# Modulation of the hybrid layers computed by GpSimd and one-column matmuls inside the feed-forwards, and the last values of stick-breaking moved

## What is computed

```python
def hybrid_layer(x, c, cos, sin, pre_g, post_g, w_ada, b_ada, w_in, w_out):
    mod = jnp.einsum('bd,de->be', jax.nn.silu(c), w_ada) + b_ada      # (1,1024) x (1024,3072)
    shift, scale, gate = jnp.split(mod, 3, axis=-1)
    h = rms_norm_2(x, pre_g) * (1 + scale[:, None, :]) + shift[:, None, :]
    ...
    return x + gate[:, None, :] * y

def swiglu(h, w_gu, w_down):                                          # the feed-forward, width 2816
    g, u = jnp.split(h @ w_gu, 2, axis=-1)
    return (jax.nn.silu(g) * u) @ w_down
```

## Time and profile before

| | us |
|---|---|
| median of three runs (1872.96 to 1873.77) | 1873.28 |
| span of the profiled execution, first to last instruction | 1873.6 |
| TensorE busy in it | 1798.3 (96%) |
| VectorE busy | 1225.3 (65%) |
| ScalarE busy | 1043.2 (56%) |
| GpSimd busy | 68.9 (4%) |
| mean granted TensorE clock | 0.985 of full |
| share of TensorE in the chain that ended last | 88% |

### The profile page before, as it was taken

One profiled execution on the slowest core, in us unless ns is written; L12 is line 12 of the kernel. 1 busy time (PEld: TensorE's weight loads), 2 busy tenths in 40 slices (PEclk: granted clock), 3 DMA queues, 4 the chain that ended last, 5 costly groups with the idle time before them and its releaser, 6 DMA issues.

```text
span 1873.6 us, 41689 instructions
## 1 busy us (share of the span) xinstructions
PE 1798.3 (96%) x17857; PEld 1616.9 (86%) x17857; DVE 1225.3 (65%) x1798; ACT 1043.2 (56%) x1625; POOL 68.9 (4%) x54
## 2 busy tenths in 40 slices
PE   7899999999999999998999999998999999999998
PEld 7798798889989888897788898897798898888887
DVE  7853567865447675498678757763577756765764
ACT  6865465555446555455665547854565544564554
POOL 0001000000000000113000000001000000000000
PEclk9999999999999999999999999999999999999998
DMA  7320255557567655545276563310356565464441
GB/s 223 113 85 3 69 183 192 185 186 243 191 222 247 202 176 189 153 155 188 65 211 199 178 199 99 115 48 4 94 185 195 175 198 174 136 204 122 136 136 67
DMA packets 288526, 287.75 MB, mean 154 GB/s; under 512 B 15240, under 2 KB 286456, under 8 KB 288344
## 3 DMA queue, kind: packets, MB, share of 16 engines
q1 hardware_dynamic: 285048, 283.98, 47.9%
q10 hardware_dynamic: 3296, 1.11, 0.3%
HBM read 284.03 MB, written 1.05 MB: 152 GB/s over the span
## 4 chain that ended last, share of the span: by engine, by line
PE 88%; DVE 4%; ACT 3%; DMA 3%; issue 2%; SPq 0%; DVEq 0%; ACTq 0%
PE ps L412 23%; PE ps L413 12%; PE ps L389 10%; PE ps L391 9%; PE ps L390 9%; PE ps L840 2%; PE ps L429 2%; PE ps L430 2%; PE ps L431 2%; PE ps L816 1%; PE ps L825 1%; PE ps L726 1%; PE ps L740 1%; PE ps L654 1%; PE ps L1009 1%
## 5 line engine op out<-in xcount | busy, mean ns | idle before, releaser
L456 DVE TENSOR_TENSOR wl<-raw,wh 128x1024 fp32r<-128x1024 f32 x484 | 584.6, 1227 | 325.2 <-ACT wh L446 318.1
L446 ACT ACTIVATE wh<-raw 128x1024 fp32r<-128x1024 f32 x484 | 498.7, 1042 | 443.5 <-PE ps L413 188.7
L412 PE MATMUL ps<-HH,wh 128*128 128x512 f32 x1408 | 489.8, 391 | 0.0
L413 PE MATMUL ps<-HH,wl 128*128 128x256 f32 x1408 | 397.0, 282 | 0.0
L412 PEld LDWEIGHTS ps<-HH,wh 128*128 128x128 f32 x1408 | 264.3, 188 | 55.6 <-issue 0.4
L389 PE MATMUL ps<-HH,wh 128*128 128x256 f32 x928 | 269.2, 290 | 6.4 <-DVE HH L2613 5.7
L413 PEld LDWEIGHTS ps<-HH,wl 128*128 128x128 f32 x1408 | 266.1, 189 | 0.1
L391 PE MATMUL ps<-HH,wl 128*128 128x256 f32 x928 | 261.2, 281 | 0.8 <-issue 0.8
L390 PE MATMUL ps<-HH,wh 128*128 128x256 f32 x928 | 261.3, 282 | 0.0
L389 PEld LDWEIGHTS ps<-HH,wh 128*128 128x128 f32 x928 | 176.8, 190 | 14.9 <-issue 5.0
L389 PE MATMUL ps<-XH,wh 128*128 128x256 f32 x576 | 166.5, 289 | 16.2 <-DVE XH L2157 9.2
(11 more groups left out here) (336 smaller groups left out, 2987.0 us busy)
## 6 DMA issues: line engine op xcount, KB each, us to landing
raw<-in_ffn_w_gu_dram SPq DMA_DIRECT2D x88, 1024.0 KB, 5.1
raw<-in_ffn_w_down_dram SPq DMA_DIRECT2D x32, 1024.0 KB, 5.2
raw<-in_w_in_dram SPq DMA_DIRECT2D x32, 1024.0 KB, 5.7
raw<-in_rw_w_rkv_dram SPq DMA_DIRECT2D x24, 1024.0 KB, 5.2
B<-in_w_ada_dram SPq DMA_DIRECT2D x24, 1024.0 KB, 8.8
raw<-in_ds_w_in_dram SPq DMA_DIRECT2D x14, 1024.0 KB, 5.3
raw<-in_ffn_w_down_dram SPq DMA_DIRECT2D x16, 768.0 KB, 4.5
raw<-in_sb_w_qkv_dram SPq DMA_DIRECT2D x12, 1024.0 KB, 5.3
```

The lines of the kernel that those rows point to most:

```text
L412: e.matmul(o[:, m, :], h_[:, k, c], x_, start=k0 + k == 0, stop=False, skip_group_check=True)
L413: i = e.matmul(o[:, m, 0:S], l_[:, k, c], x_[:, 0, :], start=False, stop=k0 + k == kt - 1, skip_group_check=True)
L446: e.activation(wh[:, u % UNITS, 0:kn * 256], raw[:, j % RAW, k0 * 256:(k0 + kn) * 256], ACT.Copy).then_inc(*up("hi"))
L456: e.tensor_tensor(wl[:, u % UNITS, 0:kn * 256], raw[:, j % RAW, k0 * 256:(k0 + kn) * 256], wh[:, u % UNITS, 0:kn * 256].bitcast(F32), ALU. ...
```

## The change

1. The 12 groups of the modulation move into the feed-forwards: 0 to 2 into the first, 3 to 6 into the second, 7 into the third, 8 to 11 into the fourth. Each group is loaded as two halves of 4 feature groups by 512 columns (1 MB each), the first behind piece 2i+2 of the gate and up pieces and the second two pieces later, where i is the pair at which the group begins.
2. GpSimd multiplies each half by silu(c) (128 x 2048), adds the feature groups (128 x 1024, then 128 x 512) and adds the two halves (128 x 512). TensorE then sums over partitions with four matmuls that have 128 columns of the sum as stationary operand and one column of -1 as the moving one; VectorE subtracts from the bias.
3. `pe_ada`, ScalarE's copies and VectorE's preparation of `scb` are gone, and so are the waits of SyncE for buffers in stick-breaking, the sparse attention and the hybrid layers.
4. In stick-breaking the first unit of the output projection is computed between `sums(3)` and `values(3)`.

```diff
+        ADA = {0: ((4, 0, 7, 9), (6, 1, 10, 7), (8, 2, 9, 10)),
+               1: ((2, 3, 7, 9), (4, 4, 10, 12), (6, 5, 7, 9), (8, 6, 10, 12)),
+               2: ((2, 7, 7, 8),),
+               3: ((2, 8, 7, 9), (4, 9, 10, 12), (6, 10, 7, 9), (8, 11, 10, 12))}
+        ADA_AFTER = {(1, 1): (("pool", ("ada", 0, 4)),), (2, 0): (("mm", ("mod", 0)),), (2, 1): (("pool", ("ada", 1, 4)),)}
+        for t_ in (5, 6, 10, 11):
+            ADA_AFTER[t_, 0] = (("pool", ("ada", t_ - 2, 4)),)
+            ADA_AFTER[t_, 1] = (("mm", ("mod", t_ - 2)),)
...
+        def ada_load(e, t, h):
+            w = wview(A["w_ada_2"][t // 6])[:, 4 * h:4 * h + 4, (t % 6) * 512:(t % 6) * 512 + 512]
+            e.dma_start(ada_half(t, h), w).then_inc(s_ada[(2 * t + h) % 8], 16)
...
+            ada_at = {first_piece["ffn", layer] + 2 * (i + h) + 3: (layer, t, h)
+                      for layer, places in ADA.items() for i, t, *_ in places for h in range(2)}
...
                 wide_block(e, ("u", layer, i), KD, h, None, ("dve", ("u", layer, i)))
-                if layer == 1 and i in (4, 8):
-                    pe_ada(e, 5 + i // 4)
-                if layer == 1 and i in (6, 10):
-                    pe_mod(e, 5 + i // 4)
+                for first, t, *_ in ADA[layer]:
+                    if i == min(first + 2, 10):
+                        pe_mod(e, t)
...
         def pe_mod(e, t):
+
             o = bank(e, ("mod", t), ("dve", ("mod", t)))
-            e.wait_ge(*at("act", ("ada", t)))
-            e.matmul(o[:, 0:4], ada_rows(t), C("sel"), start=True, stop=True,
-                     skip_group_check=True).then_inc(*up("mm", ("mod", t)))
+            e.wait_ge(*at("pool", ("ada", t, 7)))
+            for c in range(4):
+                i = e.matmul(o[:, c:c + 1], ada_half(t, 1)[:, 3, c * P:c * P + P], C("nones", 0, 1), start=True, stop=True, skip_group_check=True)
+            i.then_inc(*up("mm", ("mod", t)))
...
             values(2)
-            pe_mod(e, 2)
-            pe_ada(e, 3)
             sums(3)
-            pe_mod(e, 3)
-            pe_ada(e, 4)
+            first_out = out_units(e, layer, 0, [[("dve", ("ol", layer, k // 2))] for k in range(KD)])
+            next(first_out)
             values(3)
-            pe_mod(e, 4)
-            pe_ada(e, 5)
+            for _ in first_out:
+                pass
             cur["first"] = 0
-            pe_out_proj(e, layer, parts_of(XH, XL), [[("dve", ("ol", layer, k // 2))] for k in range(KD)])
-            pe_mod(e, 5)
+            for g in range(1, 4):
+                for _ in out_units(e, layer, g, None):
+                    pass
...
+        def pool_ada(e, t):
+
+            if t == 0:
+                e.wait_ge(*at("act", "silu c"))
+            for h in range(2):
+                w, n_ = ada_half(t, h), 2 * t + h
+                e.wait_ge(s_ada[n_ % 8], 16 * (n_ // 8 + 1))
+                e.tensor_tensor(w, w, sc_[:, 4 * h:4 * h + 4].unsqueeze(2).to_broadcast([P, 4, 512]), ALU.mult).then_inc(*up("pool"))
+                e.wait_ge(*now("pool"))
+                e.tensor_tensor(w[:, 0:2, :], w[:, 0:2, :], w[:, 2:4, :], ALU.add).then_inc(*up("pool"))
+                e.wait_ge(*now("pool"))
+                e.tensor_tensor(w[:, 0, :], w[:, 0, :], w[:, 1, :], ALU.add).then_inc(*up("pool"))
+            e.wait_ge(*now("pool"))
+            e.tensor_tensor(ada_half(t, 1)[:, 3, :], ada_half(t, 0)[:, 0, :], ada_half(t, 1)[:, 0, :], ALU.add).then_inc(*up("pool", ("ada", t, 4), ("ada", t, 7)))
+
         def pool_ffn(e, layer):
             barrier(e, "pool", ("ffn", layer))
+            for _, t, *_ in ADA[layer]:
+                pool_ada(e, t)
             pool_square(e, ("f", layer))
```

More of the change, by code:

```diff
@@ L2209, in dve_ffn @@
                     dve_angles(e)
-                if layer == 1 and i == 7:
-                    dve_mod(e, 6)
+                for first, t, *_ in ADA[layer]:
+                    if i == first + 3:
+                        dve_mod(e, t)
                 lo(e)
@@ L2219, in dve_ffn @@
             rest(10)
-            if layer == 1:
-                dve_mod(e, 7)
+            for first, t, *_ in ADA[layer]:
+                if first + 3 > 10:
+                    dve_mod(e, t)
             dve_add_x(e, "f", layer, ("norm_mix", layer + 1) if layer < 2 else None)
```

128 lines of the change are left out of this document (18 added, 110 removed).

## The result

The changed kernel takes 1971.37 us (median of 4 runs, 1969.74 to 1973.6) where the kernel before takes 1873.53 on the same chip: a ratio of 1.0529, with a 95% interval of 1.0513 to 1.0546, so 5.3% slower. The profiled span is 1970.9 us, 97.3 more than the 1873.6 of before. The forecast was 1963, with a range from 1906 to 2000. Of the runs further down, two of the ten executions of experiment 2 were disturbed (2462.8 and 6642.74 us) and stand outside its ratio; why is not known.

The account below looks back on a forecast made before the run. The prediction took TensorE's time as the program's time, with VectorE's spare limited. From 1873.6 us it took 19.0 of removed TensorE work and added 108.0 of waits for VectorE, giving 1963 us, range 1906 to 2000.

Parts of the forecast that it names:

- TensorE's work removed, 19.0: Whole program: taking out the 12 old groups' matmuls wins 19.0 us, after what TensorE then waits.
- the cover: Stick-breaking's tail: the output projection's first unit, 2.8 us, covers ScalarE's last exponentials.
- Sparse attention: 1.6 won: Sparse attention's softmax, paced by VectorE: removing two old groups wins only VectorE's waits, 0.82 each at most, 1.6 us.
- TensorE's work added, 0 of 10.8: New modulation matmuls: 0.9 us a group, 10.8 in all, taken as 0 because TensorE waits for VectorE anyway.
- GpSimd's group, 17.9: Feed-forwards: GpSimd's products and sums for one modulation group take 17.9 us, with a 128x2048 operation at 4.6.
- VectorE loses 15.7 per group: Feed-forwards: taking turns with GpSimd costs VectorE 15.7 us per group, 17.9 less 2.2.
- Lack of 10.5 per group, lead of 4.5: Feed-forwards: after 5.2 us of spare VectorE lacks 10.5 per group; a 4.5 us lead helps once per feed-forward; 108.0 together.
- The second rival: Feed-forwards: waits also drop TensorE's clock to half, and new matmuls are not free: 1994 us, chance 0.14.
- The first rival: Feed-forwards: only VectorE's subtractions take turns with GpSimd, short operations run freely: 54 us lost, 1909 us, chance 0.18.
- The faster rival: Feed-forwards: GpSimd loses the turns and works in VectorE's gaps, so only TensorE's sum counts: 1865 us, chance 0.08.
- DMA: Feed-forward loads: the moved modulation loads cost 0, being covered by two pieces in front; without cover 3 us a load.
- the DMA rival: Loads come late, 3 us each, 72 at worst: 1927 us without the turns; shares the forecast's chance of 0.58.

Follow-up runs that it names:

- experiment 2: Changed kernel with GpSimd's seven operations per group replaced by memsets of like length, so the modulation is only filled with a constant: 1871.64 us, ratio 0.9991.
- experiment 4: Changed kernel with the last values of stick-breaking put back ahead of the output projection's first unit: 1969.93 us, ratio 1.0517.
- Experiment 1: Changed kernel without GpSimd's products and sums; loads, waits and new matmuls stay: 1870.44 us, ratio 0.9977.
- experiment 6: Changed kernel with the same work spread out, groups placed further apart and some reaching into down projections: 1964.92 us, ratio 1.0493.
- 9: Experiment 5 with both products of a group back to back, after both loads: 1898.78 us, ratio 1.0147.
- Experiment 12: Experiment 10 with its groups placed anew by its trace and the first group's matmuls a pair later: 1871.95 us, ratio 0.9998.
- experiment 5: Changed kernel with GpSimd's products only, its adds left out: 1890.92 us, ratio 1.01.
- 10: Whole computation, groups spread, values first, fillers in sparse attention; GpSimd's products are one-operand 128x512, each followed by its add: 1885.69 us, ratio 1.0083.
- 11: Experiment 10 with the four products of a half first, then its three adds in a row: 1885.78 us, ratio 1.0073.
- experiment 3: Changed kernel with 32 filler matmuls on constants put into the sparse attention's softmax: 1967.35 us, ratio 1.0521.
- experiment 8: Experiment 5 with each product as four tensor_scalar operations, one tensor operand each, sums left out too: 1869.96 us, ratio 0.9986.

## Why the prediction was right

The side and the main mechanism were right: GpSimd and VectorE take turns, and TensorE waits for the subtractions. That the gate and up parts came out at 107.8 us against 108.0 was luck. They were forecast as idle time alone; they are 68.3 of idle time, some 7.8 of new matmuls and 32 of half clock, so one term was too large by 40 and two that stood at nothing in the sum made up for it. The 8 us between 1963 and 1971 are the sparse attention.

- *TensorE's work removed, 19.0.* Stick-breaking gave 13.0, as worked out, and the idle time given back in the projection was 1.01 (experiment 4 shows the row) where I had 1.3. The reason that I gave for the cover was wrong: by experiment 4 the first unit isn't needed to hide the exponentials. *Sparse attention: 1.6 won* is the step that failed outright. The stage is 6.6 us longer, with 44 us at half clock in its softmax instead of 6.8. I priced each old group by VectorE's wait behind it, and did not ask what keeps the clock up in a stretch where TensorE's matmuls are thin.
- *TensorE's work added, 0 of 10.8.* Experiment 1, where TensorE has no gaps, shows 0.6 per group in the gate and up parts, some 7.8 us in all. Whether in the changed kernel they only filled time that TensorE would have waited, as I took it, no run separates.
- *GpSimd's group, 17.9.* The extrapolated product of 128x2048 was 4.6; undisturbed it takes 3.60 (experiment 6, 666.12). The adds take 2.3 and 1.3 as forecast, and the group 15.8. *VectorE loses 15.7 per group*: 153.3 / 12 = 12.8, so about 0.8 of GpSimd's undisturbed time.
- *Lack of 10.5 per group, lead of 4.5.* With 12.8 the same sum gives 7.6 per group and 18.3 + 25.9 + 3.1 + 25.9 = 73 us; TensorE's idle time is 68.3. So the accounting by the two pairs beside a group gives about the right sum for this kernel. As a picture it was too simple, and experiment 6, expected from the same picture, missed by 89 us. I let spare time be spent whenever it comes; experiments 6 and 9 say that little more than what VectorE has during the group itself counts.
- *The second rival, the clock, at 0.14.* It was not an alternative to the forecast but an addition to it. 39.5 us more of TensorE's busy time, less the 7.8 of new matmuls, leaves 32 us lost at half clock, which is also what the granted clocks give; I had put 20 on it, and 0 in the sum. 68.3 + 7.8 + 31.7 = 107.8.
- *The first rival*, turns with subtractions only, falls by L2145's 2.89 us. *The faster rival* falls: with two tensor operands GpSimd doesn't give way. Experiment 12 shows its other side, that turns do fit into the spare once a group costs VectorE some 5.6 us (1293.5 less 1226.0, by 12) over the 33 us from its first operation to its last.
- *DMA* cost nothing: the modulation's loads land after 7.4 us, less than the 8.8 of the earlier trace rows, and experiment 1 has the same loads with no idle time. The 3 us for a load without cover should have been 3.7 by those rows (8.8 less 5.1); it stood only in the DMA rival.

One account puts these kernels in order, but it was made after most of them: TensorE's idle time per group is VectorE's loss per group, less 0.23 (VectorE's spare share, 10.5 of 44.4 us) of the time from the group's first GpSimd operation to its last, less a lead. By the traces a group extends over 26 us in the changed kernel, 19 in experiment 5, 24 in 6, 9 in 9 and 32 to 33 in 10 to 12. For the changed kernel that leaves 12.8 - 6.0 = 6.8 (5.7 measured), for experiment 5 5.5 - 4.4 = 1.1 (0.9), for 6 12.3 - 5.5 = 6.8 (4.8), for 9 6.1 - 2.1 = 4.0 (1.6), and for 10 to 12 less than nothing. So the lead is whatever is left, 0.2 to 2.4 us, and not the 4.5 that I worked out; it differs from run to run, and what sets it stays open. Experiments 9 and 11, which were meant to test an earlier form of this account, bore out its direction and not its size.

## What to carry over

Before work goes to an idle GpSimd, count its operations with two tensor operands against VectorE's spare time while they run, not against the average: an engine that feeds a short ring (here four units of weights) can save up next to nothing. If it must be done, take one-operand forms (a `tensor_scalar` for a product with a value per partition), keep two-operand ones short, and put them where VectorE has nothing else to do. And ask of every "hidden" matmul that is removed whether it keeps TensorE's clock up for the thin ones around it. In the end none of this beat the kernel before; experiment 12 is level with it.

## What the runs showed of the hardware

- GpSimd's two-operand work cost VectorE 0.8 us per us of undisturbed work (153.3 of 190) in operations of 1.3 to 3.6 us, and 0.5 to 0.6 in adds of 1.3 us (experiment 12: 67.5 of 109 with the products' share, 56.4 without the 11.1 of experiment 8). `tensor_scalar` cost it 0.06 (11.1 beside 201.2), memsets next to nothing (3.3 beside 170).
- GpSimd's `tensor_scalar` of 128x512 took 1.56 us at the least, 2.1 to 2.5 in the mean and 3.16 in the row beside two subtractions; a product of 128x2048 in one `tensor_tensor` took 3.60. The cheaper form for GpSimd is the dear one for the kernel.
- TensorE's granted clock stayed at half for 44 us in the softmax although TensorE was busy throughout (37.00 of 37.00 us). It was full again behind 64 dense records in experiment 3, but in the changed kernel it also rose at 967.7 us without any. Behind gaps of 2.64 and 3.74 us in the feed-forwards the next matmul took 0.67 and 0.76 us where 0.39 is normal.
